# A hybrid decoder layer with an expert lookup on one core: the late projections of tokens 128 to 511 beside the choice and the first expert tokens

## What is computed

```python
def time_mix(h, shift_prev, wkv0, conv_buf, ssm0, lp, chunked):
    p = h @ lp['w_in']
    p_rw = p[..., :RW_COLS]
    p_gd = p[..., RW_COLS:RW_COLS + GD_COLS]
    gates = jax.nn.sigmoid(p[..., RW_COLS + GD_COLS:])
    ya, shift_new, wkv = rwkv_branch(p_rw, shift_prev, wkv0, lp)
    yb, conv_new, ssm = gdn_branch(p_gd, conv_buf, ssm0, lp, chunked)
    ...
    merged = gates[..., :D_MODEL] * ya + gates[..., D_MODEL:] * yb
    return merged @ lp['w_out'], (shift_new, wkv, conv_new, ssm)

def gdn_branch(p, conv_buf, S0, lp, chunked):
    qkv = p[..., :GD_QKV]
    z = p[..., GD_QKV:GD_QKV + GD_WIDTH]
    ...
    qkv_c, new_buf = causal_conv(qkv, conv_buf, lp['gdn_conv_w'])
    qkv_c = jax.nn.silu(qkv_c).astype(F32)
    q, k, v = (heads(t) for t in jnp.split(qkv_c, 3, axis=-1))
    q = l2norm(q, GD_EPS) * (GD_HEAD_DIM ** -0.5)
    k = l2norm(k, GD_EPS)
    ...

def peer_ffn(x, wq, subkeys, u_tab, v_tab):
    q = (t @ wq).astype(F32).reshape(T, PEER_HEADS, 2, PEER_HALF)
    s = jnp.einsum('thpc,hpnc->thpn', q, subkeys.astype(F32))
    ...
    def apply(blk):
        x_b, e_b, g_b = blk
        hpre = jnp.einsum('tkd,td->tk', u_tab[e_b], x_b)
        return jnp.einsum('tk,tkd->td', g_b * jax.nn.gelu(hpre, approximate=False), v_tab[e_b])

def decoder_layer(x, shift_prev, wkv0, conv_buf, ssm0, lp, chunked):
    mix, st = time_mix(x, shift_prev, wkv0, conv_buf, ssm0, lp, chunked)
    x1 = layer_norm(DN_ALPHA * x + mix, lp['ln1_g'], lp['ln1_b'])
    ff = peer_ffn(x1, lp['peer_wq'], lp['peer_subkeys'], lp['peer_u'], lp['peer_v'])
    x2 = layer_norm(DN_ALPHA * x1 + ff, lp['ln2_g'], lp['ln2_b'])
```

## Time and profile before

| what | value |
|---|---|
| median of three runs | 2181.68 us (2179.1 to 2185.19) |
| profiled execution | 2167.24 us |
| its span, first to last instruction | 2165.4 us |
| DVE busy | 1334.5 us (62%) |
| PE busy | 1631.8 us (75%) |
| DMA moved | 718.93 MB, 332 GB/s over the span |
| `project` / `opening` / `running` begin at | 18 / 166 / 506.7 us |

### The profile page before, as it was taken

The page is one execution under the profiler, slowest core; times in us unless marked ns, Lnnn a source line. Parts: engine busy times, 40 slices in busy tenths (PEclk is TensorE's granted clock), DMA queues, the critical chain, the costliest instruction groups (busy, mean ns, idle before and its releaser), DMA issues. The chain is left out here.

```text
span 2165.4 us, 32160 instructions
## 1 busy us (share of the span) xinstructions
PE 1631.8 (75%) x12789; PEld 979.4 (45%) x12789; DVE 1334.5 (62%) x2996; ACT 394.7 (18%) x751; POOL 1025.7 (47%) x1091
## 2 busy tenths in 40 slices
PE   7998989895978785798787758887775655656555
PEld 7886867763655552465454415655451000100000
DVE  4296187773645468856445678474557765676745
ACT  1322423232222011124101102230101000100000
POOL 0000020004745455475455556564556777777774
PEclk9998999996989996699988859998896555555555
DMA  9215276646999999899999998999999999999997
GB/s 263 68 49 152 71 216 214 224 146 208 378 386 399 399 400 411 306 370 399 399 400 402 403 405 322 390 400 399 401 401 403 399 404 407 400 404 395 406 407 276
DMA packets 271256, 718.93 MB, mean 332 GB/s; under 512 B 29219, under 2 KB 77822, under 8 KB 270074
## 3 DMA queue, kind: packets, MB, share of 16 engines
q0 software_dynamic: 151904, 554.59, 66.2%
q1 hardware_dynamic: 116552, 161.44, 21.7%
q10 hardware_dynamic: 2650, 0.85, 0.2%
HBM read 695.58 MB, written 21.30 MB: 331 GB/s over the span
## 5 line engine op out<-in xcount | busy, mean ns | idle before, releaser
L2517 DVE CUSTOM_DVE_ANT_0 arena<-arena,ps 128x1024 f32<-128x1024 f32 x520 | 634.5, 1220 | 526.5 <-DMA arena<-peer_u_dram,arena 268.0
L2450 POOL DMA_INDIRECT arena<-peer_u_dram,arena x520 | 504.6, 970 | 488.2 <-DVE arena L2517 398.1
L2455 POOL DMA_INDIRECT arena<-peer_v_dram,arena x520 | 493.9, 950 | 162.0 <-issue 148.7
L2570 PE MATMUL ps<-arena 48*128 48x512 bf16 x1040 | 259.1, 491 | 353.7 <-DVE arena L2517 338.3
L1317 PE MATMUL ps<-arena 128*128 128x128 f32 (+1 forms) x3072 | 432.3, 297 | 59.8 <-DMA arena<-w_in_dram 26.0
L1317 PEld LDWEIGHTS ps<-arena 128*128 128x128 f32 x3072 | 393.5, 205 | 170.0 <-issue 139.1
L2583 PE MATMUL ps<-arena 128*32 128x512 f32 x2080 | 392.9, 839 | 38.9 <-DMA arena<-peer_v_dram,arena 38.7
L2570 PEld LDWEIGHTS ps<-arena 48*128 48x128 bf16 x1040 | 53.5, 97 | 640.1 <-DVE arena L2517 559.1
L2551 ACT ACTIVATE arena<-arena 128x4 f32<-128x4 f32 x130 | 26.7, 205 | 897.1 <-DVE arena L2517 896.7
L387 PE MATMUL ps<-arena 128*128 128x260 f32 (+1 forms) x704 | 130.7, 348 | 4.1 <-ACT arena L465 4.1
L387 PEld LDWEIGHTS ps<-arena 128*128 128x128 f32 x704 | 115.6, 192 | 18.2 <-ACT arena L465 4.2
(11 more groups left out here) (368 smaller groups left out, 1795.3 us busy)
## 6 DMA issues: line engine op xcount, KB each, us to landing
arena<-w_in_dram SPq DMA_DIRECT2D x40, 1024.0 KB, 13.0
arena<-peer_wq_dram SPq DMA_DIRECT2D x32, 1024.0 KB, 13.6
arena<-w_out_dram SPq DMA_DIRECT2D x16, 1024.0 KB, 12.8
arena<-w_in_dram SPq DMA_DIRECT2D x30, 512.0 KB, 4.0
arena<-peer_u_dram,arena POOLq DMA_INDIRECT x520
arena<-peer_v_dram,arena POOLq DMA_INDIRECT x520
...
```

Of the source, the lines that this page charges most:

```text
L2450: pool.indirect_dma_start(e["U"][:, k % RU, :], None, a["peer_u"][0], offsets(k)).then_inc(u_in[k % RU // UB], 16)
L2455: pool.indirect_dma_start(e["V"][:, j % RV, :], None, a["peer_v"][0], offsets(j)).then_inc(v_in[j % RV // BATCH], 16)
L2517: dve.tensor_tensor_reduce(u, u, ps[:, 0:2, :], 1.0, 0.0, ALU.mult, ALU.add, e["hp"][:, c:c + 1]).then_inc(sem("e_h"), 1)
L2570: mm = pe.matmul(ps[:, h, :], e["pick"][r, i:i + 1].to_broadcast([3 * GROUP, P]), e["xp"][r, g % 2, :], start=True, stop=True)
```

## The change

In `opening` the front runs without k and q, whose projections come after the queries and beside the choice; the convolution of k is behind the choice on DVE, and POOL issues the first six U gathers there. SP loads the slabs of z and v into parts of memory that are free by then (tile 1's input area, V slots 7 to 10). All else is in `running` and among the first 11 tokens: the convolution of q before token 0, the pieces of z, the sums, roots and reciprocals of k and q, v, its convolution, and the tails, stored by SP. The recurrence of tile 1 waits for them (`handed`), tiles 2 and 3 begin 12 and 20 tokens later, and stretches and paces of the choices are others. The layout of the per-tile inputs (`FIN`) is turned so that gv and z, which are no longer loaded for tile 1, lie in front; one store more at the start of `opening` follows from it. Operations and their shapes are otherwise the same.

```diff
-BEGINS = (-160.0, 3.0, 106.0, 224.0)
-STRETCH = (1.0, 1.0, 1.3, 1.3)
-CHOOSE_PACE = (0.55, 0.58, 0.78, 0.94, 1.2)
+BEGINS = (-160.0, 10.0, 118.0, 244.0)
+STRETCH = (1.0, 0.93, 1.0, 1.07)
+CHOOSE_PACE = (0.55, 0.5, 0.78, 0.78, 1.2)
...
-LATE_AT = dict(k=50.6, q=63.4, v=107.0, z=121.2)
-LATE_CT = dict(k=2.25, q=2.25, v=2.25, z=2.25)
+LATE_AT = dict(k=88.6, q=104.5)
+LATE_CT = 2.25
...
+SEQUENCE = [("f", i) for i in range(16)] + [("keys", 0)] + [("f", i) for i in range(16, NSLAB)] + [("k", 0), ("k", 1), ("q", 0), ("q", 1)]
+LATE_UNITS = [(g, ct) for g in "kq" for ct in range(4)] + [("z", 0), ("z", 1)] + [(g, ct) for g in ("kn", "qn") for ct in range(4)] + [
+    ("z", 2), ("z", 3)] + [(g, ct) for g in "vc" for ct in range(4)]
...
@@ def arrived
         eng.wait_ge(m["sem"]("x1_saved"), 16 * 13 * n)
+    if n == 1:
+        handed(m, eng)
...
-L_AT = dict(kn=72.3, qn=82.0, conv=116.2, tails=131.0)
+Z_AT, V_AT, KN_AT, QN_AT, CONV_AT, TAILS_AT = (-1.5, -0.6, 0.7, 1.7), (2.7, 3.7, 4.7, 5.7), -0.38, -0.3, 6.7, 8.7
...
+def late_piece(m, pe, g, ct, slabs):
+    late_free(m, pe, g, ct)
+    for h in range(2):
+        for k in range(4):
+            mm = pe.matmul(m["ps"][:, late_bank(g, ct), 0:NL_], slabs[h][:, k, ct * P:(ct + 1) * P], m["xT"][:, 4 * h + k, P:NP],
+                           start=(h == 0 and k == 0), stop=(h == 1 and k == 3))
+    mm.then_inc(m["sem"]("b_mm"), 1)
...
+            late_piece(m, pe, g, ct, [ring[number % SLOTS] for number in numbers])
+            if (g, ct) == ("q", 1):
+                pe.wait_ge(m["sem"]("s_done"), 2)
+                pe.wait_ge(m["sem"]("sel_done"), 2)
+                turn_chosen(m, pe, front(m, 0))
...
+def late_dve(m, dve):
+    yield begins(0) + 118.0
+    opened(m, dve)
+    for ct in range(4):
+        late_convolve(m, dve, "k", ct)
+
+def late_slabs(m, sp):
+    sp.wait_ge(m["sem"]("s_wkv_out"), 32)
+    for g in "zv":
+        for h in range(2):
+            sp.dma_start(m["lb"][g + "slab"][h], late_source(m, g, h)).then_inc(m["sem"]("b_slab_" + g), 16)
+
+def late2_pe(m, pe):
...
+    yield from gate(0)
+    yield from gate(1)
+    yield from sums("k", KN_AT)
+    yield from sums("q", QN_AT)
+    yield from gate(2)
+    yield from gate(3)
...
+def late2_act(m, act):
...
+    yield from squares("k", 1, -1.6)
+    yield from gate(0)
+    yield from squares("q", 2, -0.7)
+    yield from gate(1)
+    yield from roots("k", KN_AT)
+    yield from roots("q", QN_AT)
...
+def late2_dve(m, dve):
+    sem, lb, st = m["sem"], m["lb"], m["front_steps"]
+    yield -1.5
+    for ct in range(4):
+        late_convolve(m, dve, "q", ct)
+    for g, at in (("k", 0.1), ("q", 1.1)):
         conv, sq = lb["conv"][g], lb["sq"][g]
         for half in range(2):
+            yield at + 0.1 * half
             h = slice(2 * half, 2 * half + 2)
             dve.wait_ge(sem("b_out"), taken(late_number(g + "n", 2 * half + 1)))
             st.link(dve.reciprocal(sq[:, h], sq[:, h]))
...
+def handed(m, eng):
+    sem = m["sem"]
+    eng.wait_ge(sem("b_out"), taken(len(LATE_UNITS)))
+    eng.wait_ge(sem("b_unit"), 2)
+    for name, tiles in (("gk", 3), ("gq", 3), ("gv", 2)):
+        eng.wait_ge(sem("b_spilled_" + name), 16 * tiles)
+    eng.wait_ge(sem("tail_out"), len(TAILS))
+    eng.wait_ge(sem("tails_saved"), 64)
...
@@ def opening, gpsimd
+            pool.wait_ge(sem("sel_taken"), 2)
+            pool.wait_ge(sem("x1_saved"), 16 * 13)
+            for k in range(RU):
+                gather_u(m, pool, k)
...
@@ def experts_pool
+            if j == 6:
+                pool.wait_ge(sem("b_spilled_z"), 16 * (NT - 2))
+            elif j == 7:
+                pool.wait_ge(sem("b_mm"), late_number("v", 3))
...
@@ def running
+            in_turn(experts_sp(m, sp), late2_sp(m, sp), *(s(m, sp, n) for n in later for s in (fin_sp, front_sp, store_sp) if (s, n) != (fin_sp, 1)), states_sp(m, sp), rows_sp(m, sp))
...
+            in_turn(late2_act(m, act), experts_act(m, act), *(s(m, act, n) for n in later for s in (recur_r_act, recur_g_act, front_act)),
...
+            in_turn(experts_dve(m, dve), late2_dve(m, dve), *(s(m, dve, n) for n in later for s in (recur_r_dve, recur_g_dve, front_dve)),
...
+            in_turn(late2_pe(m, pe), experts_pe(m, pe), *(s(m, pe, n) for n in later for s in (recur_r_pe, recur_g_pe, front_pe)),
```

More of the change, by code:

```diff
@@ L1963, in taken @@
 def taken(u):
[L1965 to L1985 removed]
+    return u + sum(g in "zc" for g, _ in LATE_UNITS[:u])
@@ L1998, in project_late, with late_act @@
-            mm.then_inc(done, 1)
-    def sums(g):
+            late_piece(m, pe, g, ct, [ring[number % SLOTS] for number in numbers])
[3 more added lines that the diff above has]
+                turn_chosen(m, pe, front(m, 0))
+def late_act(m, act):
+    sem, lb, ps = m["sem"], m["lb"], m["ps"]
+    for g in "kq":
+        raw, row = lb["raw"][g], LATE_ROW[g]
         for ct in range(4):
-            yield begins(0) + L_AT[g + "n"] + 0.3 * ct
+            yield begins(0) + LATE_AT[g] + LATE_CT * (ct + 0.95)
+            act.wait_ge(sem("b_mm"), late_number(g, ct))
@@ L2003, in sums @@
             if ct == 0:
-                pe.wait_ge(sem("b_sq"), 1 if g == "k" else 2)
-            free(g + "n", ct)
-            pe.matmul(ps[:, bank(g + "n", ct), 0:NL_], const(m, "ones"), lb["sq"][g][:, ct], start=True, stop=True).then_inc(done, 1)
-    yield from project_late("k")
-    yield from project_late("q")
-    yield from sums("k")
-    yield from sums("q")
-    yield from project_late("v")
-    for ct in range(4):
-        yield begins(0) + L_AT["conv"] + 1.2 * ct
-        pe.wait_ge(out, taken(late_number("v", ct)))
-        if ct == 0:
-            pe.wait_ge(sem("b_taps"), 16)
-        free("c", ct)
-        for tap in range(4):
-            mm = pe.matmul(ps[:, bank("c", ct), 0:NL_], lb["taps"][:, 4 * ct + tap], lb["raw"][1][:, ct, tap:tap + NL_], start=(tap == 0), stop=(tap == 3))
-        mm.then_inc(done, 1)
@@ L2022, in late_pe @@
-    yield from project_late("z")
-    for n, (j0, j1, _) in enumerate(TAILS):
-        yield begins(0) + L_AT["tails"] + 0.5 * n
-        if n == 0:
-            pe.wait_ge(out, taken(late_number("z", 3)))
-            pe.wait_ge(sem("b_tail"), 3)
-        else:
-            pe.wait_ge(sem("tail_out"), n)
-        for j in range(j0, j1):
-            mm = pe.transpose(ps[0:TAIL, 2 + (j - j0) // 4, (j - j0) % 4 * P:((j - j0) % 4 + 1) * P], m["tail"][:, j, :], const(m, "ident"))
-        mm.then_inc(sem("tail_mm"), 1)
@@ L2095, in late_act @@
         if ct == 0:
             act.wait_ge(sem("b_spilled_gk"), 16 * (NT - 1))
-        act.wait_ge(done, late_number("c", ct))
-        act.activation(fin1[:, FIN["gv"] + ct], ps[:, bank("c", ct), 0:P], ACT.Silu).then_inc(out, 1)
-        act.activation(lb["conv"]["v"][:, ct, P:], ps[:, bank("c", ct), P:NL_], ACT.Silu).then_inc(out, 1)
-    yield from take("z")
+        act.wait_ge(sem("b_mm"), late_number("c", ct))
+        act.activation(fin1[:, FIN["gv"] + ct], ps[:, late_bank("c", ct), 0:P], ACT.Silu).then_inc(sem("b_out"), 1)
@@ L2101, in late_act @@
+        act.activation(lb["conv"]["v"][:, ct, P:], ps[:, late_bank("c", ct), P:NL_], ACT.Silu).then_inc(sem("b_out"), 1)
     for n, (j0, j1, first) in enumerate(TAILS):
-        yield begins(0) + L_AT["tails"] + 0.5 * n + 0.4
+        yield TAILS_AT + 0.5 * n + 0.05
         act.wait_ge(sem("tail_mm"), n + 1)
```

344 lines of the change are left out of this document (174 added, 170 removed).

## The result

The changed kernel takes 2187.94 us (median of 20 runs, 2173.61 to 2197.98), the kernel before 2179.09 us (median of 20, 2168.74 to 2185.19). The ratio is 1.0043, with a 95% interval of 1.0029 to 1.0057: slower by about 9 us. The forecast was no change (+0.6 us), the range 2162 to 2198.

A forecast was written before the change was run, and what follows sets the result against it. The prediction took the tokens to be bound by their gathers. Its terms, -43.4 + 47 + 2 + 4 + 3 - 12 = +0.6 us on a median of 2181.7, gave 2182, no measurable change; range 2162 to 2198.

The forecast's parts named there:

- three of the prediction's signs: Choice starts at 375 to 385, `running` begins at 460 to 466; token 11 before 540 or after 560 means wrong.
- One sign: Among the first tokens, v's pieces take about 5.2 us each at a granted clock near 1.
- The opening: Before the token block: without k and q the choice starts 33 us earlier; with what follows, -43.4 us.
- The first tokens: Tokens up to the eleventh wait on the late projections; token 11 at about +87 against 39.6: +47 us.
- the clock: Among the first tokens, v may start at PE's low clock: +3 us, bounds 0 and +20.8.
- The stores' wait and the recurrence: Tile 1's recurrence waits for the tails' stores, +2 us, and now lies on tokens 12 to 17, +4 us.
- The collisions: Recurrences of tiles 2 and 3 leave the choices before them, stretches that lose 27 us: -12 us.
- the slower one: First tokens: v's pieces, v's convolution and the tails run at PE's low clock; 2200, chance 0.16.
- The rival of the opening that does not become shorter: Opening: output projection slabs hold the front, so the choice starts only 20 us sooner; 2195, chance 0.12.
- The faster one: Later tokens: all 27 us come back, and tile 1's recurrence finds PE at full clock; 2160, chance 0.36.

The follow-up runs named there:

- the run with ln and exp: Changed kernel with roots and reciprocals of k and q made on ACT as ln and exp: 2172.85 us, ratio 0.9992.
- the two runs with the table alone and without it: New begins, stretches and pace of tiles 2 and 3 put into the kernel before: ratio 0.9971; undone in the changed kernel: 1.0066.
- without the wait: Tile 3 at token 246, stretch 1.0: in the changed kernel 0.9968; in the kernel before, with tile 2 at 118 and pace 0.78, 0.9914.

## Why the prediction missed by 8 us

The range held and the forecast of no change did not: the time moved a little to the slow side. By the times of the trace three of the prediction's signs came out late: the choice starts at 389.74 for 385 at most, `running` at 474.65 for 466, and token 11 at 564.08, past the 560 that was to show the prediction wrong. 8.8 us of each is the early part (the load at 279.16 for 270.35); without it they are 380.9, 465.8 and 555.3, within the bounds. One sign failed outright: v's first piece took 8.15 us in place of 5.2. Term by term:

- **The opening, -43.4 us: measured -39.9.** The size was nearly right, the reason in part. From the samples' first load to the choice it is 110.6 us (279.16 to 389.74) in place of 141.5, so 31 us, where 33 were forecast. The prediction had DVE's chain hold the front of the kernel before. Two runs each take a part of DVE's work out and leave PE's (taps and reciprocals), and in neither the choice comes earlier. What is left are PE's 43 us of k's and q's pieces with the slabs that they wait for; these two go together and were not tried apart. In the changed kernel the prediction's chain is there: PE waits 15.4 us in all for DVE's steps L1512 and L1520, which stand among the samples' steps, and 8.49 us for a slab, which fits that only 31 of the 43 us are won.
- **The first tokens, +47 us and +3 for the clock: measured +49.8** (89.4 - 39.6). Token 0 was put at +13, the reciprocals at +19, token 2 at +45, token 11 at +87; the rows give 13.9, 17.6, 43.1 and 89.4. That DVE's reciprocals lie on this chain is shown by the run with ln and exp; the clock's share was 2 us by the run that kept PE busy.
- **The stores' wait and the recurrence, +2 and +4: measured +8.5** (tokens 11 to 17, 23.5 us for 15.0). The wait was 1.30 us. The rest is the recurrence, which I had put down by 2 us for the low clock it had in the kernel before; it ran at 0.67 again.
- **The collisions, -12 us: measured -5 to -6** by the two runs with the table alone and without it. In the profile shown it is -12.1 (18.7 us late at token 104, 6.6 at the end), just the forecast, but that is luck: tokens 268 to 280 ran at 0.86 there, and in the second profile, at 0.73, it is -6.5. This is the term that failed by the executions as a whole. The denser work does take back the 21 us counted above, but without the wait 18.7 us are left in the kernel before and, by 1.0066 against 0.9968, 21 us in the changed one, more than the forecast. The prediction counted DVE's work per token in the new order and did not ask which instruction of ACT now stands behind which. Token 244 puts the recurrence's copy behind a layer norm, PE waits 3.64 us, and what follows the wait takes away two thirds of the gain or more.

The terms as measured add up to +13 us with the collisions at -5 to -6, and with -12.1, and 0.3 between tokens 17 and 104, to the profile's 6.6; the medians differ by 9.

The rivals: the slower one had the right mechanism at the wrong place. Among the first tokens the low clock is there but costs 2 us, not the 18 that make its 2200, since of v's four pieces only the first was slow and the slow pieces of z lie beside DVE's reciprocals. What follows a wait at token 270 costs more. The Trainium skill, "TensorE: Matmul & The Clock Gate", section "HAM oscillation — how this bites in real kernels", says that bursts between waits start cold; the traces agree for the pieces of z and v behind a wait (8.15 us for 5.43) and for token 270. The rival of the opening that does not become shorter falls (the choice came 31 us sooner, not 20). The faster one, 2160, falls too; without the wait the changed kernel takes 2172, still 12 us above it.

On the table loads the trace of this case decides against the price of the Trainium skill, "ScalarE: Activation LUTs", section "What ACT_TABLE_LOAD costs": the rows above have the load at 1421.39 for 1.28 us and the next activation at 1422.69, with no drain in between.
